# Two transformer blocks on one core: three modulation chunks placed later in the weight queue and on the engines

## What is computed

```python
# first block, its end
z = rms_norm(h, ffn_norm_gain) @ w_ff1          # 1024 x 4096
h = h + jnp.square(jax.nn.relu(z)) @ w_ff2      # 4096 x 1024
# second block
mod = jnp.dot(silu(c), w_ada) + b_ada           # 1024 x 6144
sh1, sc1, g1, sh2, sc2, g2 = jnp.split(mod, 6)
h = rmsnorm(x, norm_mix) * (1.0 + sc1) + sh1
proj = jnp.dot(h, w_in)                         # 16 chunks of 512 columns
...
x = x + g1 * jnp.dot(merged, w_out)
h2 = rmsnorm(x, norm_ffn) * (1.0 + sc2) + sh2
y = hierarchical_moe(h2, ...)
x = x + g2 * y
```

## Time and profile before

| | before |
|---|---|
| device time of three runs | 1162.31, 1162.40 and 1166.04 us; median 1162.4 |
| span of the profiled execution | 1160.9 us; the rest, some 1.5 us, lies around it |
| TensorE busy | 1130.3 us, 97% of the span |
| VectorE, ScalarE, GpSimd busy | 53%, 44%, 17% |
| chain that ended last | TensorE 81%, DMA 7%, VectorE 6%, GpSimd 3%, ScalarE 2% |
| bytes read from HBM | 329.83 MB, 285 GB/s over the span |

### The profile page before, as it was taken

How to read it: one execution, slowest core, us unless ns; L and a number is a source line. 1 busy time by engine, 2 the same in 40 slices (tenths; PEclk the granted TensorE clock), 3 DMA queues, 4 the chain that set the end, 5 groups by cost and what they waited for, 6 DMA issues and landing times.

```text
span 1160.9 us, 18111 instructions
## 1 busy us (share of the span) xinstructions
PE 1130.3 (97%) x7361; PEld 865.5 (75%) x7361; DVE 613.5 (53%) x885; ACT 515.0 (44%) x849; POOL 196.0 (17%) x132
## 2 busy tenths in 40 slices
PE   8999999999799899999999999999999999999996
PEld 7988878999688788878888886666666666666664
DVE  6989767789864696596466643222222222222223
ACT  6666353744465374854655433223222233222223
POOL 1339860124442331400000000000000000000000
PEclk9999999999899899999999999999999999999999
DMA  9952642576556666565366479999999999999994
GB/s 322 286 184 73 227 145 97 197 286 225 213 216 233 203 198 193 187 218 174 133 201 260 175 264 418 425 421 421 425 423 422 427 422 422 427 422 422 424 423 185
DMA packets 82698, 332.01 MB, mean 286 GB/s; under 512 B 4555, under 2 KB 6926, under 8 KB 66110
## 3 DMA queue, kind: packets, MB, share of 16 engines
q1 hardware_dynamic: 81236, 328.43, 73.0%
q0 software_dynamic: 1088, 2.34, 1.0%
q10 hardware_dynamic: 298, 0.11, 0.0%
HBM read 329.83 MB, written 1.05 MB: 285 GB/s over the span
## 4 chain that ended last, share of the span: by engine, by line
PE 81%; DMA 7%; DVE 6%; POOL 3%; ACT 2%; issue 1%; DVEq 0%; SPq 0%; ACTq 0%; POOLq 0%
PE bank L1087 17%; PE bank L441 12%; PE bank L442 12%; PE bank L443 12%; PE bank L1106 9%; PE bank L1077 5%; DMA ring<-in_w_exp_down 3%; POOL ring L2644 3%; DMA ring<-in_w_ada 2%; PE bank L568 2%; DVE ring_r L1820 2%; PE bank L1134 1%; PE bank L1135 1%; ACT ring L1398 1%; PE bank L1094 1%
## 5 line engine op out<-in xcount | busy, mean ns | idle before, releaser
L1820 DVE TENSOR_TENSOR ring_r<-ring,arena_r 128x2048 fp32r<-128x2048 f32 x93 | 224.6, 2424 | 130.8 <-ACT arena_r L1307 129.2
L1307 ACT ACTIVATE arena_r<-ring 128x2048 fp32r<-128x2048 f32 x93 | 177.2, 1916 | 148.7 <-PE bank L443 66.8
L2644 POOL TENSOR_TENSOR ring<-ring 128x512 f32<-128x512 f32 x84 | 149.0, 1797 | 234.6 <-ACT ring L1398 205.6
L443 PE MATMUL bank<-arena_r,actT_r 128*128 128x512 f32 x384 | 150.5, 392 | 0.0
L441 PE MATMUL bank<-arena_r,tok_r 128*128 128x512 f32 x352 | 140.9, 400 | 1.7 <-DVE con L2285 1.7
L442 PE MATMUL bank<-ring_r,tok_r 128*128 128x512 f32 x352 | 138.2, 393 | 0.0
L2457 DVE TENSOR_TENSOR arena<-bank,arena 64x512 f32<-64x512 f32 x62 | 42.7, 689 | 175.4 <-PE bank L1106 174.7
L441 PE MATMUL bank<-tok_r,arena_r 128*128 128x256 f32 x352 | 99.5, 283 | 1.8 <-DVE actT_r L1837 1.2
L443 PE MATMUL bank<-tok_r,ring_r 128*128 128x256 f32 x352 | 98.3, 279 | 0.0
L442 PE MATMUL bank<-actT_r,arena_r 128*128 128x256 f32 x352 | 98.2, 279 | 0.0
L2443 DVE TENSOR_TENSOR arena<-bank,arena 128x256 f32<-128x256 f32 x32 | 13.6, 425 | 149.8 <-ACT arena L1739 93.8
(11 more groups left out here) (424 smaller groups left out, 1830.3 us busy)
## 6 DMA issues: line engine op xcount, KB each, us to landing
ring<-in_w_in SPq DMA_DIRECT2D x22, 2048.0 KB, 9.3
ring<-in_w_exp_down SPq DMA_DIRECT2D x22, 2048.0 KB, 21.3
ring<-in_w_exp_gate SPq DMA_DIRECT2D x21, 2048.0 KB, 22.0
arena<-in_w_exp_up SPq DMA_DIRECT2D x21, 2048.0 KB, 23.5
ring<-in_w_ff SPq DMA_DIRECT2D x16, 2048.0 KB, 8.7
ring<-in_w_ada SPq DMA_DIRECT2D x12, 2048.0 KB, 11.2
arena<-in_w_exp_gate SPq DMA_DIRECT2D x11, 2048.0 KB, 21.6
arena<-in_w_exp_down SPq DMA_DIRECT2D x10, 2048.0 KB, 21.5
```

Of the source, the lines that this page charges most:

```text
L443: return mm(o, l[1], r[0], start=False, stop=stop)
L1307: A(hi, w, ACT.Copy).then_inc(S["w_high"], 1)
L1820: TT(half(i, ringR)[0], w, hi.bitcast(fp32), ALU.subtract).then_inc(S["w_rest"], 1)
L2644: i = nc.gpsimd.tensor_tensor(w[:, k, :], w[:, k, :], w[:, k + n, :], ALU.add)
```

## The change

The load of chunk 7 moves from behind product 0 of the second feed-forward matrix to behind product 1, that of chunk 8 from behind product 3 to behind 4, and that of chunk 9 from behind product 6 to behind product 0 of the second block's `w_in`. TensorE's and VectorE's part moves behind product 2, product 5 and step 0. ScalarE's scaling of chunk 7 moves from the first feed-forward layer to behind the first `w_high` of product 2, that of chunk 8 to product 5, and that of chunk 9 behind the last `w_high` before the norm. GpSimd no longer waits for `z_done` before chunk 7. The arithmetic is the same.

```diff
-        ADA_FF2 = {0: 7, 3: 8, 6: 9}
-        ADA_STEP = {3: 10, 6: 11}
-        ADA_Z = {1: 5, 6: 6, 12: 7}
-        ADA_HALF = {("ff2", 3, 0): 8, ("ff2", 6, 0): 9}
+        ADA_FF2 = {2: 7, 5: 8}
+        ADA_STEP = {0: 9, 3: 10, 6: 11}
+        ADA_Z = {1: 5, 6: 6}
+        ADA_HALF = {("ff2", 2, 0): 7, ("ff2", 5, 0): 8, ("win2", 0, 1): 9}
...
-        ADA_BEHIND = {..., ("ff2", 0): (7,),
-                      ("ff2", 3): (8,), ("ff2", 6): (9,), ("win2", 2): (10,), ("win2", 6): (11,)}
+        ADA_BEHIND = {..., ("ff2", 1): (7,),
+                      ("ff2", 4): (8,), ("win2", 0): (9,), ("win2", 2): (10,), ("win2", 6): (11,)}
...
-                    if c == 7:
-                        pool.wait_ge(S["z_done"], 14)
                     scaled[0] += 1
                     pool.wait_ge(S["c_silu"], scaled[0])
```

More of the change, by code:

```diff
@@ L293, in program @@
                  + [("ff1", c) for c in range(8)] + [("ff2", c) for c in range(8)] + steps2)
-        ADA_BEHIND = {("win", 2): (0,), ("win", 6): (1, 2, 3, 4), ("ff1", 2): (5,), ("ff1", 5): (6,), ("ff2", 0): (7,),
-                      ("ff2", 3): (8,), ("ff2", 6): (9,), ("win2", 2): (10,), ("win2", 6): (11,)}
+        ADA_BEHIND = {("win", 2): (0,), ("win", 6): (1, 2, 3, 4), ("ff1", 2): (5,), ("ff1", 5): (6,), ("ff2", 1): (7,),
+                      ("ff2", 4): (8,), ("win2", 0): (9,), ("win2", 2): (10,), ("win2", 6): (11,)}
         order = []
```

## The result

| | before | after |
|---|---|---|
| device time, median of 4 runs each | 1162.4 us | 1171.4 us (1170.7 to 1172.3) |
| ratio, 95% interval | | 1.0074 [1.0057, 1.009] |
| span of the profiled execution | 1160.9 us | 1169.1 us |

What follows compares the result with a forecast made beforehand. TensorE, 97% busy, was bounded by its waits for GpSimd's additions (chunks 7, 9) and the low clock behind. Forecast: -3.7 + 4.2 = +0.5, plus 2.5 for the clock, +3.0; 1160.9 + 3.0 + 1.5 = 1165.4 us, range 1157.5 to 1170.5.

Steps and rivals of the forecast that it cites:

- The times up to chunk 7's additions: First feed-forward's end into the second matrix: sine begins at 311.3, GpSimd starts chunk 7 at 320.0, leaving out `z_done` costs nothing.
- The norm: Second block's start: new 2.5 us wait, GpSimd's additions slow VectorE by 2.0; product 0 ends at 414.3, 3.7 ahead.
- the estimate by it of 4 us: At the norm: each hit VectorE operation waits out one addition of up to 2 us, making the forecast 1167.4.
- Step 1: Second block after product 0: chunk 10's load, scaling and additions delay the second rotary tile; loss 4.2 to 6.0, taken 4.2.
- the parts on chunks 7 and 8: Second feed-forward matrix: additions take 15 us each; chunk 7 keeps a 2.3 us wait and chunk 8 has none.
- one fall of the clock: New waits of 2.5, 1.9 and about 2 us: one lowers TensorE's clock, up to 3.4 us, net 2.5.
- The sum hangs little on chunk 7: Chunk 8 in the second feed-forward matrix: had chunk 7 not waited, chunk 8 would wait 3 us.
- Rival 3: Slower: clock falls in each new wait and additions take 17 us; +8.5, 1170.9, down to +5.5; 27%.
- a sum of +0.5 us: Whole change before any clock fall is charged: -3.7 at the second block's product 0, +4.2 in its step 1.
- The gap of 1.2 us: TensorE idle from 511 to 514 us before the change, clock staying at 1.00; taken as a gap too short to lower it.

## Why the prediction was wrong

Part of its steps stand, and two came out right in size by luck. **The times up to chunk 7's additions** are right: sine at 311.75 (forecast 311.3), GpSimd from 320.44 (320.0). `z_done` cost nothing: GpSimd starts when the scaling ends.

**The norm**: its wait is right, 2.67 us (2.5). Its stretch, 403.30 to 413.73, is 1.7 us longer than before where I had said 2.0, but I had laid it to GpSimd's additions beside VectorE. The kernel with chunk 9 alone moved has the same additions there (393.13 for 9.24 us) and a clock of 1.00, and its stretch is 404.88 - 395.79 = 9.1 us, only 0.3 longer than before. The other 1.3 us come with the low clock (0.83) behind the wait. The Trainium skill ("SBUF — State Buffer", "Who interferes with whom") had VectorE wait out whole additions there; one operation of 0.42 us took 1.52 and the next 0.75, which agrees with waits of up to one addition of 1.3 us, but TensorE waited for neither. What was too much is the estimate by it of 4 us, with 2 us for an addition. The skill's rule on which operations collide agrees with every row here: rests and other operations with two inputs in SBUF are slowed, and the scalar operations of the angles too, those that read a bank are not.

**Step 1** takes the forecast time for another reason: from the end of product 0 to the end of the second rotary transposes 450.79 - 422.45 = 28.3 us (28.6), a loss of 3.9 against 24.4 where I took 4.2. The forecast had VectorE's L2294 set it, ready 27.9 us after product 0. It was ready at 448.08 + 0.42, after 26.1 us, and TensorE came at 449.75 and did not wait for it. What took the time is the bank wait of 1.94 us, sized right, and the low clock behind it: 3.4 us at 1.2 instead of 2.4 GHz, 1.7 us lost. The wait for L2294 comes out once the bank wait is removed.

**The step that failed** is in the parts on chunks 7 and 8: "Its seven additions took 13.5, 14.5 and 17.0 us, the more the more VectorE works beside them; I take 15." I had the direction and took a middle value for both, without counting what would lie beside them. The 17.00 us of the earlier trace rows would have told me: VectorE's timeline of the kernel before has four rests beside them and the start of a fifth, and where both chunks were to go, ScalarE makes four or five high parts on end.

```profile
373.31 9.62 DVE L1820 TENSOR_TENSOR ring_r<-ring,arena_r 128x2048 fp32r<-128x2048 f32 x3 [7.83 <-ACT arena_r L1307]
385.17 2.32 DVE L1820 TENSOR_TENSOR ring_r<-ring,arena_r 128x2048 fp32r<-128x2048 f32 x1 [2.24 <-ACT arena_r L1307]
387.73 3.04 DVE L1820 TENSOR_TENSOR ring_r<-ring,arena_r 128x2048 fp32r<-128x2048 f32 x1 [0.24 <-ACT arena_r L1307]
```

Counted, the rows give a sum: 9.1 us alone (9.16, 9.05), 13.1 beside two rests, 15.0 and 15.1 beside three, 17.0 beside four, 19.0 beside five; (19.0 - 9.1) / 5 = 2.0 us for each whole rest. Smaller operations with two inputs in SBUF add to it: the 14.54 us of the earlier trace rows lie beside two rests and six operations on activations. By moving chunk 7's scaling behind product 2's first conversion the change puts five conversions' rests beside the additions. That cost 4.0 us at chunk 7 and 2.0 at chunk 8 (17.0 for 15).

**Why 4 + 2 us were not caught up**: chunk 8's load hangs on chunk 7's transposes, and chunk 9's stands behind one that hangs on chunk 8's. Chunk 8's chain is longer than the three products between (from 340.65 to 377.72, 37.1 us against 33.3), and chunk 9's holds up the squares. So the lateness is handed on. Against the forecast:

| | forecast | measured | off |
|---|---|---|---|
| chunk 7's transposes done | 336.2 | 340.6 | +4.4 |
| chunk 8's | 372.7 | 378.9 | +6.2 |
| norm transposes begin | 394.6 | 403.3 | +8.7 |
| product 0 ends | 414.3 | 422.45 | +8.2 |
| second rotary transposes end | 442.9 | 450.8 | +7.9 |

Of the 2.5 us that come on at the norm, 2.1 are chunk 9's load, second of a pair: it landed 16.1 us after its issue, and the earlier trace rows had 14.1 and 13.9. This pair begins with a chunk of `w_in`, and its first load is late too, 11.3 us. The forecast charged 2.5 us for one fall of the clock on top of this table; in the trace the falls at the norm and at the bank (0.83 in both windows) lie inside the measured stretches, where the forecast had put GpSimd's additions and L2294 in their place. So the whole is 8.2 - 3.0 = 5.2 us above the forecast, and not 7.9.

**"The sum hangs little on chunk 7"** failed too. It was argued for an earlier chunk 7; in the table a later one is handed on whole, and where angles and sine stand behind and chunk 7 is done 7.0 us earlier, chunk 8's transposes are done 5.1 us earlier. The experiment with chunk 7 alone, where chunk 8 stands off that chain, is 4.9 us faster than before.

**Rival 3** named the time (1170.9) and both of its conditions held: additions of 17 us or more and a lower clock in the new waits. Its reckoning is not what happened, though, and that its time was met is luck: it gave the additions 1.5 us where chunk 7's and 8's cost 6, and it added three falls of the clock to a sum of +0.5 us in which the falls at the norm and the bank, 1.3 and 1.7 us, turned out to stand already, under other names. The Trainium skill's rule on TensorE's clock ("TensorE: Matmul & The Clock Gate", "What's actually happening"), which I had leaned that rival on, agrees with the windows of 0.83 and 0.66 behind the changed kernel's four new or longer waits. But neither whether the clock falls nor for how long follows from the wait alone: it was low for 6.8 us behind 2.79 us in the changed kernel, for 3.3 behind 5.70 in the kernel with angles and sine behind (0.89 on the mean from 366 to 381 us), for 10.2 behind 6.55 in that with chunk 8 scaled first, and not at all behind 2.73 us in that with chunk 7 scaled a product later. Its window of 374 to 384 us, and then that of 394 to 404 us around the wait of 1.33 us with chunk 9 alone moved. The gap of 1.2 us in the earlier trace rows is the part of the 1.66 us wait near 512 us that lies in that window:

```profile
374.00:384.00 10.00, 7.27 (x34) 5.71 (x33) 6.24 (x4) 2.79 (x2) 4.58 (x3) 1.00 0.35 92
```

```profile
394.00:404.00 10.00, 8.64 (x45) 6.75 (x45) 7.29 (x15) 6.22 (x19) 8.22 (x7) 1.00 0.22 66
```

Open: why chunk 9's pair of loads took 16.1 us rather than 14 (16.2 and 16.0 in two more kernels with the same pair), and how much of the 8.2 us a change of chunk 7 and 8 without 9 would cost, which was not run. That the additions' length comes from the rests beside them is shown by moving them (9.05, 13.14, 15.01, 19.01 us for one chunk). What happens within one operation can be read from the single additions: one of 1.3 us becomes one of 3.2 to 3.3 for each whole rest of 2.29, and the rest grows by up to 1.1, as if each waited out what was left of the other.

## What to carry to other kernels

When work on one engine is moved, count what will lie beside it on the engine that it disturbs, and price it from rows with the same count, not from the mean of its rows. In a ring of slots, draw the chain from load to load: items as far apart as the ring is long hang on one another, and if the chain from load to release is longer than the work between them, delays are handed on. More distance between load and use mended it here, and for one chunk a shorter chain did, its scaling ahead of another item's conversion; moving load and use together didn't. And when a forecast has the right size for a stretch, see in the trace whether the cause named is the one that is there. A freed engine's time is worth only what the next thing in its program order leaves of it (here the angles and the sine).

## What the runs showed of the hardware

GpSimd's seven additions of 128x512 cost 9.1 us alone and about 2.0 us more for each 128x2048 rest that VectorE makes beside them, one addition of the seven growing from 1.3 to 3.3 us for each, while each such rest grows from 2.29 to some 3.2 us: both sides lose. With VectorE's scalar operations beside them (the angles) the additions took 9.05 us, no longer than alone, and only VectorE lost, 1.12 to 4.97 us for four small operations, 1.0 us for each. Which side pays depends on the operation. Behind waits of TensorE of 1.9 us and more its clock was mostly at 1.2 GHz, for 3.4 to 10.2 us, but behind one of 2.73 us it stayed at 2.4 GHz, as behind those of 1.33 and 1.65; the length of the wait did not say which.
